# An empty first turn in TensorE's expert loop, token transposes split six and four around the second down product, and a shorter tail, in a fused decoder block

## The reference, cut to what matters

```
logits = xn @ router_w + router_b;  top 4 of 32, gates = softmax(top_vals)
for expert e, its tokens xb:
    h = xb @ gu_w[e] + gu_b[e]                      # 1024 -> 2 x 1024
    x_glu, x_lin = min(h[:, 0::2], 7), clip(h[:, 1::2], -7, 7)
    act = x_glu * sigmoid(1.702 * x_glu) * (x_lin + 1)
    y[tokens] += gate * (act @ dn_w[e] + dn_b[e])
out = rms_norm(h_mixer + y, norm_final_w)
```

## Time and profile before

| | us |
|---|---|
| median of 3 runs | 2271.7 (2269.38 to 2271.95) |
| the profiled execution, its own time | 2272.49 |
| its span, first to last instruction | 2270.4 |
| TensorE busy | 2200.7 (97%) |
| VectorE busy | 1259.6 (55%) |
| granted TensorE clock, mean | 0.99 |

### The profile page before, as it was taken

One profiled execution on the slowest core, in us unless ns is written; L12 is line 12 of the kernel. 1 busy time (PEld: TensorE's weight loads), 2 busy tenths in 40 slices (PEclk: granted clock), 3 DMA queues, 4 the chain that ended last, 5 costly groups with the idle time before them and its releaser, 6 DMA issues.

```text
span 2270.4 us, 49537 instructions
## 1 busy us (share of the span) xinstructions
PE 2200.7 (97%) x19222; PEld 1600.0 (70%) x19223; DVE 1259.6 (55%) x2504; ACT 478.9 (21%) x988; POOL 350.2 (15%) x360
## 2 busy tenths in 40 slices
PE   8999998899999998999999999999999999999997
PEld 3444444888445776888678877788777887788775
DVE  6466533455434455556655665556655665556664
ACT  3233001444333111111111111111111111111113
POOL 0000001121022211111112211122111221121112
PEclk9999999999998999999999999999999999999998
DMA  3111112333533767888878988689877998679987
GB/s 143 50 60 47 51 61 64 96 104 123 192 131 104 310 254 279 304 301 309 333 272 298 344 303 308 253 324 340 307 301 263 333 350 325 254 292 334 349 300 260
DMA packets 120628, 535.01 MB, mean 236 GB/s; under 512 B 27795, under 2 KB 61735, under 8 KB 87776
## 3 DMA queue, kind: packets, MB, share of 16 engines
q1 hardware_dynamic: 98416, 489.30, 56.2%
q0 software_dynamic: 22160, 44.98, 7.8%
HBM read 485.24 MB, written 40.05 MB: 231 GB/s over the span
## 4 chain that ended last, share of the span: by engine, by line
PE 92%; DMA 3%; issue 2%; DVE 2%; POOL 0%; ACT 0%; SPq 0%; POOLq 0%; DVEq 0%
PE ps L2145 41%; PE ps L2194 17%; PE ps L1654 9%; PE ps L1752 5%; PE ps L2025 5%; PE ps L2177 2%; PE ps L1851 2%; PE ps L2229 1%; PE ps L1701 1%; PE ps L1860 1%; DMA idx_g<-list_s 1%; PE ps L1833 1%; PE ps L1865 1%; DMA arena<-xn_s,idx_g 1%; PE ps L1953 1%
## 5 line engine op out<-in xcount | busy, mean ns | idle before, releaser
L2145 PE MATMUL ps<-arena 128*128 128x128 f32 (+2 forms) x8192 | 994.2, 284 | 10.3 <-issue 8.9
L2145 PEld LDWEIGHTS ps<-arena 128*128 128x128 f32 x8192 | 986.2, 192 | 22.9 <-issue 21.2
L2194 PE MATMUL ps<-arena 128*64 128x512 f32 x1984 | 393.3, 544 | 9.9 <-DVE arena L1554 9.7
L1508 DVE TENSOR_TENSOR arena<-arena 128x1024 f32<-128x1024 f32 x248 | 294.3, 1217 | 0.0
L2194 PEld LDWEIGHTS ps<-arena 128*64 128x64 f32 x1984 | 134.2, 137 | 218.9 <-issue 193.9
L1495 DVE TENSOR_SCALAR arena<-ps,arena 128x160 f32<-128x160 f32 x256 | 97.9, 382 | 321.3 <-PE ps L2145 320.0
L1027 ACT ACTIVATE arena<-arena 128x160 f32<-128x160 f32 x256 | 86.1, 336 | 815.9 <-DVE arena L1495 815.9
L1654 PE MATMUL ps<-arena 128*128 128x512 f32 x448 | 195.7, 594 | 0.0
L730 POOL DMA_INDIRECT sum_s<-arena,idx_s x31 | 51.5, 1662 | 851.9 <-ACT arena L1042 851.9
L1654 PEld LDWEIGHTS ps<-arena 128*128 128x128 f32 x448 | 84.5, 190 | 109.4 <-issue 109.4
L1752 PE MATMUL ps<-arena 128*128 128x512 f32 x280 | 120.6, 592 | 0.8 <-ACT arena L871 0.8
(11 more groups left out here) (280 smaller groups left out, 2088.6 us busy)
## 6 DMA issues: line engine op xcount, KB each, us to landing
arena<-gu_w SPq DMA_DIRECT2D x128, 2048.0 KB, 11.5
arena<-dn_w SPq DMA_DIRECT2D x128, 1024.0 KB, 11.2
arena<-dn_b SPq DMA_DIRECT2D x32, 512.0 KB, 15.4
arena<-w_in_t SPq DMA_DIRECT2D x26, 512.0 KB, 3.2
arena<-arena SPq DMA_DIRECT2D x50, 256.0 KB, 2.7
arena<-w_out SPq DMA_DIRECT2D x2, 2048.0 KB, 7.9
arena<-x SPq DMA_DIRECT2D x8, 512.0 KB, 5.1
xn_s<-arena SPq DMA_DIRECT2D x8, 512.0 KB, 2.8
```

Source lines behind the costliest of these rows:

```text
L1508: nc.vector.tensor_tensor(dst[:, w, :], a[:, w, :], b[:, w, :], op).then_inc(s_ds, 1)
L2145: last = nc.tensor.matmul(ps[:, f % 2, k * C:k * C + size], wslot[u][:, kt, o:o + P], xT[:, kt, 0:size], start=kt == 0, stop=kt == KT - 1, ...
L2194: last = nc.tensor.matmul(ps[rows, bank, 0:width], acts[:, k, :], weights[:, k, :], start=first and k == 0, stop=k == K2 - 1, skip_group_c ...
```

## The change

- TensorE's first loop runs 33 turns instead of 32. The first does neither down product nor transposes (`k > 0` fails) and finds class 0 as `need`, so it passes all conditions and does nothing. A row of `size_i` holds the turn numbers (0, 0, 1, ... 31), since `turn` is now read from it, and the sizes stand one place further on. The wait for the sizes is now ahead of the loop.
- The first six transposes stay ahead of `down_second`; the last two of `xg` and the two of `xg2` come behind it.
- The second half of `down_third` goes to bank 5, which the token transposes use and ACT has copied by then, instead of bank 6; it waits for that copy and no longer for DVE's read of bank 6. DVE reads its last two quarters from bank 5. The wait for the half sums (`s_as`) is moved to the start of `down_third`.
- In the tail the ten transposes for expert 32, POOL's list load and gather for it, and ACT's copies are gone. DVE's L1594 and L1595 stand behind the five scaled tiles.

```diff
-        size_i = sb("size_i", [P, ROUNDS, E + 2], I32)
+        size_i = sb("size_i", [P, ROUNDS + 1, E + 3], I32)
...
             def last_rows_out():
                 n = E - 1
-                gather(E, 0, E)
                 pool.wait_ge(s_sc, 32 * n)
...
                     nc.scalar.activation(sum_of(t), sum_of(t), ACT.Copy, scale=stat3[:, 2, t:t + 1]).then_inc(s_sd, 1)
-                copy_xT(E)
...
-            nc.vector.memset(size_i[:, :, :], 0)
+            ch.link(nc.vector.memset(size_i[:, :, :], 0))
...
                 if t == 0:
+                    ch.link(nc.vector.tensor_copy(size_i[:, ROUNDS, 1:E + 1], iexp))
...
-            nc.vector.tensor_copy(size_i[:, :, 1:E + 1], size_f).then_inc(s_sz, 1)
+            nc.vector.tensor_copy(size_i[:, 0:ROUNDS, 2:E + 2], size_f).then_inc(s_sz, 1)
...
-                    nc.vector.tensor_tensor(Yt[lower, HALF:HALF + PW], Yt[lower, HALF:HALF + PW], ps[lower, 6, 0:PW],
+                    nc.vector.tensor_tensor(Yt[lower, HALF:HALF + PW], Yt[lower, HALF:HALF + PW], ps[lower, 5, 0:PW],
                                             ALU.add)
-                    nc.vector.tensor_tensor(Yt[lower, HALF + PW:D], y_both[upper, PW:HALF], ps[upper, 6, 0:PW], ALU.add
+                    nc.vector.tensor_tensor(Yt[lower, HALF + PW:D], y_both[upper, PW:HALF], ps[upper, 5, 0:PW], ALU.add
...
-                dve.wait_ge(s_ls, 16 * TT * TOPK + 32)
-                dve.wait_ge(s_db, 16 * (PIECES + 1) * (n + 1))
-                dve.wait_ge(s_is, 32 * n + 32)
-                nc.vector.scalar_tensor_tensor(out=rows, in0=dnb, scalar=gate, in1=rows, op0=ALU.mult, op1=ALU.add)
-                nc.vector.scalar_tensor_tensor(out=rows2, in0=dnb2, scalar=gate2, in1=rows2, op0=ALU.mult, op1=ALU.add)
                 dve.wait_ge(s_sq2, 2 * TT)
...
                 for t in range(ACT_TILES, TT):
                     scaled_tile(t)
+                dve.wait_ge(s_ls, 16 * TT * TOPK + 32)
+                dve.wait_ge(s_db, 16 * (PIECES + 1) * (n + 1))
+                dve.wait_ge(s_is, 32 * n + 32)
+                ch.link(nc.vector.scalar_tensor_tensor(out=rows, in0=dnb, scalar=gate, in1=rows, op0=ALU.mult, op1=ALU.add))
+                ch.link(nc.vector.scalar_tensor_tensor(out=rows2, in0=dnb2, scalar=gate2, in1=rows2, op0=ALU.mult, op1=ALU.add))
...
             def down_third(n, m, q, o):
                 pe.wait_ge(s_ds, 8 * q + 8 + 8)
+                pe.wait_ge(s_as, 5 * q + 5 + 5)
                 pe.wait_ge(s_xe, 3 * m + 4)
                 pe.wait_ge(s_ye, o + 7)
                 both((2, a_sum, d_dif, False), (4, a22, d_all, True), True)
-                pe.wait_ge(s_as, 5 * q + 5 + 5)
-                pe.wait_ge(s_ye, o + 8)
-                both((6, a_all, d22[:, :, 0:PW], True), (6, a_all, d22[:, :, PW:HALF], True), True)
+                pe.wait_ge(s_xe, 3 * m + 5)
+                both((5, a_all, d22[:, :, 0:PW], True), (5, a_all, d22[:, :, PW:HALF], True), True)
...
-                for kt in range(4 * part, 4 * part + 4):
+                for kt in range(6 * part, 6 + 2 * part):
...
-                with pe.Fori(0, E if isinstance(r, int) else E + 1) as turn:
-                    n, m = r * E + turn - 1, r * (E + 1) + turn
+                def down_and_transposes(turn, size, n, m):
                     o, q = five(n, r), summed(n, r)
                     with pe.If(turn > 0):
                         down_first(n, q, o)
-                    size = size_at(turn)
                     transpose_tokens(m, 0)
-                    transpose_tokens(m, 1)
                     with pe.If(turn > 0):
                         down_second(n, q, o)
+                    transpose_tokens(m, 1)
...
-                    pe.wait_ge(s_sz, 2)
-                    need = size_at(turn + 1)
+                pe.wait_ge(s_sz, 2)
+                first = isinstance(r, int)
+                with pe.Fori(0, E + 1) as k:
+                    if first:
+                        turn = pe.value_load(size_i[0:1, ROUNDS, bass.ds(k, 1)], min_val=0, max_val=E - 1)
+                        n, m = turn - 1, turn
+                        with pe.If(k > 0):
+                            down_and_transposes(turn, size_at(k), n, m)
+                        need = size_at(k + 1)
...
                     down_half(n, 0)
-                    for part in range(2):
-                        transpose_tokens(m, part)
```

More of the change, by code:

```diff
@@ L419, in five, with tokens_of @@
             return 5 * n if isinstance(r, int) else 5 * n - 2
+        def tokens_of(r):
+            return 0 if isinstance(r, int) else r * (E + 1) - 1
         def summed(n, r):
@@ L721, in rows_out @@
                 n = r * E + e
-                gather(e + 1, r, r * (E + 1) + e + 1)
+                gather(e + 1, r, tokens_of(r) + e + 1)
                 if not free:
@@ L786, in expert_rows @@
                 else:
-                    gather(0, r, r * (E + 1))
+                    gather(0, r, tokens_of(r))
                     with pool.Fori(0, E) as e:
@@ L1029, in expert_act @@
             def expert_act(r):
-                copy_xT(r * (E + 1))
+                copy_xT(tokens_of(r))
                 with act.Fori(0, E - 1 if isinstance(r, int) else E) as e:
@@ L1034, in expert_act @@
                         glu_sigmoid(n, f)
-                    copy_xT(r * (E + 1) + e + 1)
+                    copy_xT(tokens_of(r) + e + 1)
                     act.wait_ge(s_is, 32 * n + 32)
@@ L2227, in transpose_tokens @@
                     pe.wait_ge(s_gx, 16 * m + 16)
-                for kt in range(4 * part, 4 * part + 4):
+                for kt in range(6 * part, 6 + 2 * part):
                     last = nc.tensor.transpose(ps[:, 4 + kt // 4, kt % 4 * P:(kt % 4 + 1) * P], xg[:, kt * P:(kt + 1) * P],
                                                ident)
-                last.then_inc(s_xt, 1)
+                    if kt % 4 == 3:
+                        last.then_inc(s_xt, 1)
                 if part == 1:
@@ L2258, in expert_pe @@
                         down_third(n, m, q, o)
-                    pe.wait_ge(s_sz, 2)
-                    need = size_at(turn + 1)
+                pe.wait_ge(s_sz, 2)
[7 more added lines that the diff above has]
+                        need = size_at(k + 1)
+                    else:
+                        n, m = r * E + k - 1, r * (E + 1) + k - 1
+                        down_and_transposes(k, size_at(k + 1), n, m)
+                        need = size_at(k + 2)
                     with pe.If(need == 3):
@@ L2273, in expert_pe @@
                 if isinstance(r, int):
-                    n, m = E - 1, E
-                    size = size_at(E)
+                    n = E - 1
+                    size = size_at(E + 1)
                     down_half(n, 0)
-                    for part in range(2):
-                        transpose_tokens(m, part)
                     with pe.If(size > 1):
@@ L2286, in expert_pe @@
                     nc.tensor.matmul(ps[:, 0, 0:1], stack_all, rows_sq[:, 2:3], start=True, stop=True).then_inc(s_rank, 1)
-                pe.wait_ge(s_xe, 3 * (r + 1) * (E + 1) + 3)
+                pe.wait_ge(s_xe, 3 * (r + 1) * (E + 1))
             pe.addr_align(FETCH_BLOCK, offset=1, max_nops=0)
```

## The result

The changed kernel is slower: 2284.5 us median (2280.3 to 2286.1, 5 runs) beside 2272.0 for the kernel before (5 runs), a ratio of 1.0050, 95% interval 1.0039 to 1.0061. The forecast was 2263.5, with a range to 2272. The profiled execution took 2286.1 us, its span is 2284.2, 13.8 longer than before.

A forecast was written before the change was run, and what follows sets the result against it. TensorE, busy 97% of the span, was taken to bound the kernel. Empty turn -1.2, six/four -4.3 and tail -2.7 sum to -8.2 us on 2272.5, giving 2264.3, forecast as 2263.5 against the median; range 2257 to 2272.

The forecast's parts named there:

- wait for the first transposes: Ahead of the first expert on TensorE: the empty turn makes the transposes start 11.0 us late, between 5.5 and 13.3.
- lower clock behind it: After TensorE's idle time in the empty turn, the lower clock is paid once more, 1.8 us.
- three holes gone: Gate/up products: three idle gaps from code coming in, with half clock after each, vanish, saving 14.0 us.
- register loads in every turn: Expert loop: registers and loads were counted only in the empty turn, 0.4 us, with nothing for later turns.
- six/four: Ten transposes split around the second stretch: 16 class 1 turns 0.38 us shorter, 15 others 0.12 longer, together -4.3 us.
- tail: After the last gate/up: scaled tiles and row writes start earlier, moving L753 by -2.7 us, bounds -0.7 and -3.5.
- the empty turn's delay: Loop start: three jumps to absent code at 4.8 us plus 0.4, partly under the warm-up, delay the transposes 11.0 us.
- The guess of the cover: At the holes, queued products hide some 2 us of each jump, giving an upper end of 5.6 us a jump.
- the forecast's likeliest case: All three holes go and the time lands at 2260 to 2267.5 us; chance 0.49.
- the free bank: Second half of the third stretch no longer waits for DVE's read of bank 6; worth 0.
- The slower rival: Empty turn is pure cost: the three holes come back on top of 12.8 us, +5.8, 2277.5 us; chance 0.07.

The follow-up runs named there:

- g2: The changed kernel with the wait for the sizes moved from ahead of the loop to the second turn: 2275.6 us, ratio 1.0014 to the kernel before.
- f1: The changed kernel with its expert loop begun at the second turn, so the empty turn is not run: 2263.0 us, ratio 0.9956 to the kernel before.

## Why the prediction was wrong

The table splits the difference of the two profiled spans, 13.8 us, into the prediction's terms. A hole's worth is read as the excess of its leg, or of its whole turn, over the same in later turns of the class. The first term is taken from start to start: the first transpose begins 24.0 us behind the last warm-up product now, and 0.4 before.

| term | forecast | in the trace |
|---|---|---|
| wait for the first transposes | +11.0 | +23.8 (24.0 - 0.4, +0.2 up to the first gate/up) |
| lower clock behind it | +1.8 | +1.7 (first leg 36.71, clean 34.97) |
| three holes gone | -14.0 | -14.2 (5.07 + 2.24 + 1.63 + 3.65 + 1.57) |
| register loads in every turn (the rest of the loop) | 0 | +4.2 (16 x 0.19, 15 x 0.08) |
| six/four (by the trace of it alone) | -4.3 | -3.8 |
| tail | -2.7 | -1.3 |
| everything ahead of the warm-up | 0 | +3.2 |
| sum | -8.2 | +13.6 |

**The price of a jump.** The step that failed is the empty turn's delay, 3 x 4.8 + 0.4 us less what the warm-up covers: forecast 11.0, measured 23.8, past its upper end of 13.3. The larger part is the jump. The prediction took 4.8 us with an upper end of 5.6, from the hole plus a guess of 2 us of cover. The branch records show 6.2, 7.2 and 8.2. The guess of the cover was not bad: the records before say 5.5, 3.6 and 4.8 in full. But the holes were the cheap cases. The instruction queue's rows and the windows over the six jumps sort them:

| | DMA share about 1 | DMA share 0.26 to 0.46 |
|---|---|---|
| one fetch in the branch | 5.5 (before), 6.2 (empty turn) | 3.6 (before) |
| two fetches | 7.2, 8.2 (empty turn) | 4.8 (before) |

A fetch moves 16 KB (0.49 MB in 30 packets) through DMA engines that, at the loop's start, are busy with the experts' weights (348 to 399 GB/s in the windows). By the packets' own times in the trace, the first fetch starts 3.9, 3.0 and 4.0 us after the branch in the empty turn, and 2.7, 1.0 and 0.7 us after it at the three holes; one fetch takes 0.9 to 2.2 us, and from the end of the last fetch to the end of the branch it is 1.4 to 1.9 us in all six. So most of what the empty turn's jumps cost more lies ahead of the fetch, and not in the sequencer afterwards. The same jumps in the other kernels took 5.5 to 6.4, 3.3 to 3.7, 4.7 to 5.1 and 7.4 to 8.2 us, in the order first hole, second hole, third hole, last two of the empty turn; only g2 differs, with 3.82 and 2.32 us at the jump over the down code and the first far one. That the DMA traffic is the cause is read from these, not shown: no kernel fetched at the same place with the queues quiet. 7.1 of the 12.8 us of error in this term (23.8 - 11.0) are the three jumps, 21.5 us instead of 14.4.

The Trainium skill, "Runtime: NRT & Kernel Launch", section "Instruction fetch mechanics", says that a taken branch to code outside the window forces a fetch before execution goes on. The trace agrees: 6.2 to 8.2 us for each such branch in the empty turn. The prediction drew a stall in every turn from that section's two cache lines, and none came: every later branch at these lines took 0.21 us at most. That was also a partial reading: the same section of the Trainium skill gives 128 KiB for TensorE's instruction memory, which is more than the two lines of 16 KiB. No run here measures that size.

**What the turn executes.** Forecast 0.4 us for registers and loads. The records have 2.5 us from the wait's end to the first far branch (742.22 to 744.68), and 3.1 from the end of the third (766.32) to the first transpose, which is the next turn's head. These 5.2 us beyond the forecast are nearly all of the rest of that error. The turn did start some 4 us ahead of the warm-up's end, as forecast, but 2.5 of these went to loads. The two empty turns put the same price on it: 3.6 for a turn without a fetch.

**The loads in later turns.** The prediction counted the new loads only in the empty turn. They stand in all 32 turns, ahead of the product that TensorE needs next, and cost 0.2 us in a class 1 turn. That is a step left out, and worth more than the six/four change brought.

**The holes.** Right in size, with all three gone as the forecast's likeliest case had it. But a part of the credit isn't the empty turn's: begun at the second turn, the same loop has lost the third hole too, so that the 14.0 came out is in part luck. In this program the empty turn bought 8.6 us (the two holes of f1) for 25.5; with the 3.3 us by which f1's turns are shorter that makes 20.2 of the 21.5 us between the two medians.

**Six/four.** Right in mechanism and size: -0.38 a class 1 turn, as worked out; +0.20 instead of +0.12 in the others; and 0.7 us more from the one long turn, -3.8 in all. In the changed kernel itself a class 1 turn is only 0.17 us shorter, outside the 0.3 to 0.45 that the prediction named, because the loads and the new branch take 0.2 of it back. No idle time shows for the free bank.

**The tail.** The gain in the chain was 3.3 (forecast 2.7), and the drain gave back 2.2. The prediction followed the chain to L753 and not to the last instruction of the program. It also took the two edits as one saving, where either has it alone.

**Ahead of the warm-up.** +3.2 us here, yet the kernel with two empty turns has the same code ahead and ended its warm-up 3.8 us earlier than the kernel before. So it looks like scatter of an execution and not like the change; one profile of each does not settle it.

**The rival.** The slower rival had the sign, by another mechanism: it had the holes stay. They went, and the cost itself was twice the size.

## What to carry to other kernels

A first visit to code is cheap where products are queued and dear where nothing is: 2 to 4 us seen of a jump in the running loop, 6 to 8 us each in the empty turn, where weights were streaming in besides. Touching code early pays only under cover as long as the fetches, so read the branch records in the view of a source line, which give the whole price and not the part that shows. Whatever is added to a loop's head for one special turn is paid in all of them, and a saving at the end counts only if it is followed to the program's very last instruction.

## What the runs showed of the hardware that was not expected

- A branch to absent code took 3.3 to 3.7 us with one fetch and little DMA traffic and up to 8.2 with two fetches beside 350 to 400 GB/s; the same branch later 0.07 to 0.2 us.
- TensorE's sequencer was 2.0 us ahead of the products at the loop's branch in the turn read above. Two register loads of 0.30 us, with their steps and branches, used this up and cost 0.2 us a turn.
- TensorE had no product from 746.0 to 769.45. The granted clock was 0.50 in the windows from 750.92 to 766.30 and again in the first gate/up products, from 772.80 to 775.30; from 775.50 to 779.00 it was 0.96.
- GpSimd's last drain took 1.87 us in the nine programs with the dead gather and 4.08 in the seven without, the same to the hundredth each time.
- Whether a piece of code was still there at its second use went with two edits together (six/four and a shift of three instructions): without the empty turn, the three kernels with both lack the branch of 4.7 to 5.1 us, and the nine with one or none have it.
